# GpSimd for the low halves of the merged branches, and other places for ten weight panels, in a two-block transformer kernel

## The reference: two transformer blocks

```python
proj = h @ w_in[layer]                       # low-rank inputs, q, k, v of three attentions, gate logits
q = _rmsnorm(q, mla_q_norm_g[layer])         # per head, then rotary turning; k, and the differential
k = _rmsnorm(k, mla_k_norm_g[layer])         # attention's q1, q2, k1, k2 likewise
...
gates = jax.nn.sigmoid(gate_logits + gate_b[layer]).reshape(b, p_len, N_BRANCHES, d)
merged = (gates[:, :, 0] * (out_a @ wb_a.T)
          + gates[:, :, 1] * (out_b @ wb_b.T)
          + gates[:, :, 2] * (out_c @ wb_c.T))
h_res = h_res + merged @ w_out[layer]
```

## Time and profile before

| | |
|---|---|
| median of 3 runs | 3101.68 us (3100.57 to 3109.37) |
| the profiled execution's own time | 3117.64 us |
| its span | 3115.8 us |
| PE busy | 3059.5 us (98%) |
| DVE, ACT, POOL busy | 1938.5 us (62%), 1277.4 us (41%), 204.3 us (7%) |
| mean granted PE clock | 0.985 of full speed |

### The profile page before, as it was taken

The page is one execution under the profiler, slowest core; times in us unless marked ns, Lnnn a source line. Parts: engine busy times, 40 slices in busy tenths (PEclk is TensorE's granted clock), DMA queues, the critical chain, the costliest instruction groups (busy, mean ns, idle before and its releaser), DMA issues.

```text
span 3115.8 us, 46880 instructions
## 1 busy us (share of the span) xinstructions
PE 3059.5 (98%) x16677; PEld 2556.8 (82%) x16677; DVE 1938.5 (62%) x3719; ACT 1277.4 (41%) x2142; POOL 204.3 (7%) x350
## 2 busy tenths in 40 slices
PE   9999999999999999999999999999999999999999
PEld 7667899976779888888888888788888888877888
DVE  5555656654567787555576557755556555645775
ACT  4436565343565744222232443322223222345443
POOL 0000000000000010101010001111110111112000
PEclk9999999999999999999999999999999999999999
DMA  4222345622224564444453114455554445532454
GB/s 181 82 75 82 116 176 198 216 90 77 82 90 159 189 233 136 144 148 143 146 177 120 55 56 162 137 159 159 155 158 136 156 155 155 154 106 89 142 188 156
DMA packets 122707, 431.12 MB, mean 138 GB/s; under 512 B 16176, under 2 KB 19504, under 8 KB 122048
## 3 DMA queue, kind: packets, MB, share of 16 engines
q1 hardware_dynamic: 93776, 336.28, 31.3%
q0 software_dynamic: 26880, 86.47, 9.4%
q10 hardware_dynamic: 1904, 6.36, 0.6%
HBM read 427.99 MB, written 8.85 MB: 140 GB/s over the span
## 4 chain that ended last, share of the span: by engine, by line
PE 64%; DMA 3%; DVE 2%; ACT 1%; issue 1%; DVEq 0%; SPq 0%; ACTq 0%
PE ps L446 14%; PE ps L447 14%; PE ps L448 14%; PE ps L458 7%; PE ps L460 3%; DMA modraw<-in_mod 2%; PE ps L563 1%; PE ps L564 1%; PE ps L565 1%; PE ps L981 1%; PE ps L494 1%; PE ps L492 1%; PE ps L578 1%; PE ps L503 1%; DMA raw<-in_panels 1%; PE ps L957 1%
## 5 line engine op out<-in xcount | busy, mean ns | idle before, releaser
L1081 ACT ACTIVATE whi<-raw 128x1024 fp32r<-128x1024 f32 x632 | 668.8, 1058 | 1305.3 <-PE ps L448 808.4
L1679 DVE TENSOR_TENSOR wlo<-raw,whi 128x1024 fp32r<-128x1024 f32 x632 | 776.0, 1228 | 607.7 <-ACT whi L1081 578.5
L446 PE MATMUL ps<-xs,whi 128*128 128x512 f32 (+2 forms) x2248 | 794.5, 353 | 4.5 <-DVE wlo L1679 4.1
L448 PE MATMUL ps<-xs,wlo 128*128 128x512 f32 (+2 forms) x2248 | 780.5, 347 | 0.0
L447 PE MATMUL ps<-xs,whi 128*128 128x512 f32 (+2 forms) x2248 | 779.7, 347 | 0.0
L446 PEld LDWEIGHTS ps<-xs,whi 128*128 128x128 f32 x2248 | 427.3, 190 | 82.1 <-issue 26.4
L447 PEld LDWEIGHTS ps<-xs,whi 128*128 128x128 f32 x2248 | 427.8, 190 | 51.1 <-issue 1.0
L448 PEld LDWEIGHTS ps<-xs,wlo 128*128 128x128 f32 x2248 | 427.2, 190 | 49.8
L404 POOL DMA_DIRECT2D modraw<-in_mod x288 | 155.1, 538 | 2525.6 <-DVE modsum L1786 2359.7
L446 PE MATMUL ps<-hidden,whi 128*128 128x512 f32 (+2 forms) x838 | 294.9, 352 | 0.0
L448 PE MATMUL ps<-hidden,wlo 128*128 128x512 f32 (+2 forms) x838 | 294.8, 352 | 0.0
(11 more groups left out here) (392 smaller groups left out, 4552.1 us busy)
## 6 DMA issues: line engine op xcount, KB each, us to landing
raw<-in_panels SPq DMA_DIRECT2D x632, 512.0 KB, 3.3
modraw<-in_mod POOLq DMA_DIRECT2D x288, 256.0 KB, 3.0
bias_by_column<-in_rpb POOLq DMA_DIRECT2D x16, 476.2 KB, 8.0
bia<-bias_by_column POOLq DMA_DIRECT2D x32, 96.0 KB, 2.6
rtab<-in_rtab ACTq DMA_DIRECT2D x2, 1312.0 KB, 7.6
wuq<-in_wuq ACTq DMA_DIRECT2D x2, 768.0 KB, 6.3
con<-in_con SPq DMA_DIRECT2D x1, 1345.5 KB, 12.0
h<-in_x SPq DMA_DIRECT2D x1, 1088.0 KB, 6.5
```

What stands on the lines that cost most here:

```text
L446: pe.matmul(out, w_hi, x_hi, start=start, stop=False)
L448: return pe.matmul(out, w_lo, x_hi, start=False, stop=stop)
L1081: act.activation(whi[:, s * PW:(s + 1) * PW], raw[:, s * PW:(s + 1) * PW], ACT.Copy).then_inc(hi_split, 1)
L1679: dve.tensor_tensor(wlo[:, s * PW:(s + 1) * PW], raw[:, s * PW:(s + 1) * PW], whi[:, s * PW:(s + 1) * PW].bitcast(F32), ALU.subtract).then ...
```

## The change

It has four parts.

1. The 16 subtractions that make `mlo` (8 for each layer) go from DVE to GpSimd. Those of layer 0 stand ahead of all modulation loads in GpSimd's queue, those of layer 1 ahead of load 18. DVE now waits, ahead of the first branch of pairs 2 and 3, until GpSimd has finished with the half of `mrg` that it will write.
2. `SPREAD_FILL` goes from (4, 9, 14, 19) to (4, 9, 14, 23): filler 15 runs behind all spreads.
3. `UNIT_FILL` goes from (1, 3, 5, 7, 11, 15, 18, 20, 22) to (-1, 2, 4, 6, 9, 12, 15, 18, 21): filler 0 runs ahead of unit 0, and the other eight lie two or three units apart.
4. As a consequence of 1, the first two modulation loads are issued when layer 0's merged chunks are done, not at the start.

```diff
-UNIT_FILL = (1, 3, 5, 7, 11, 15, 18, 20, 22)
-UNIT_FILLS, SPREAD_FILL = len(UNIT_FILL) + 3, (4, 9, 14, 19)
+UNIT_FILL = (-1, 2, 4, 6, 9, 12, 15, 18, 21)
+UNIT_FILLS, SPREAD_FILL = len(UNIT_FILL) + 3, (4, 9, 14, 23)
...
+            def merged_lo(layer, m):
+
+                T, at = width1(layer), (m % 4) * T1
+                pool.wait_ge(part_hi, layer * (NC + FF1) + m + 1)
+                pool.tensor_tensor(mlo[:, m * T1:m * T1 + T], mrg[:, at:at + T], mhi[:, m * T1:m * T1 + T].bitcast(F32), ALU.subtract).then_inc(part_lo, 1)
+            for m in range(NC):
+                merged_lo(0, m)
+            first_layer_halves = 16
 
 
             n_halves = 2 * DEPTH * MODT
             for k in range(n_halves):
+                if k == first_layer_halves + 2:
+                    for m in range(NC):
+                        merged_lo(1, m)
                 s = k % 2
...
+                filler(0)
                 for u, (tens, i, p0, p1, z) in enumerate(us):
...
-                    if u in UNIT_FILL:
+                    if u in UNIT_FILL[1:]:
                         filler(UNIT_FILL.index(u))
...
-                def merged_lo(mp):
-                    for j in range(2):
-                        m, at = 2 * mp + j, (mp % 2 * 2 + j) * T1
-                        lane.take(part_hi)
-                        dve.tensor_tensor(mlo[:, m * T1:m * T1 + T], mrg[:, at:at + T], mhi[:, m * T1:m * T1 + T].bitcast(F32), ALU.subtract).then_inc(part_lo, 1)
-                    lane.count(part_lo).add(2)
+                lane.count(part_hi).add(NC)
...
                     if br == 0:
                         lane.take(gate_ready)
-                        lane.settle(part_lo)
+                        if mp > 1:
+                            lane.count(part_lo).add(2)
+                            lane.settle(part_lo)
...
-                    if br == 1 and mp:
-                        merged_lo(mp - 1)
-
...
-                merged_lo(NC // 2 - 1)
+                lane.count(part_lo).add(4)
```

## The result

| | kernel before | changed kernel |
|---|---|---|
| median of 5 runs each | 3102.71 us | 3086.68 us (3083.91 to 3090.82) |
| ratio | | 0.9944, 95% interval 0.9932 to 0.9957 |
| timed again, with the last experiments | 3107.40 us (17 runs) | 3090.14 us (6 runs), 0.9941 (0.9929 to 0.9953) |
| profiled execution: own time, span | 3117.64, 3115.8 us | 3090.82, 3089.0 us |

The change gains 16 us by the medians, 17 and 18 by the two ratios (0.0056 and 0.0059 of 3105 us). Forecast were 3082 and a gain of 20. The profiled executions differ by 26.8 us, more than the timed ones: the one of before was 15 us slower than its kernel's median. So I don't read gains from this pair alone but place by place, over the traces of all the kernels that share a place.

A forecast was written before the change was run, and what follows sets the result against it. PE bounds the kernel, its waits costing idle time and then a low clock. Terms of 22.0 us less 2.0 gave 20.0; 3101.7 less that is 3081.7, forecast 3082, range 3074 to 3096.

The forecast's parts named there:

- The start: ACT's first square: x lands earlier without two modulation loads in GpSimd's queue; 0.9 us gained, at most 1.2.
- Units: Key and first units: first-square waits and three low clock stretches go; 2.6 us in layer 0, 4.1 in layer 1.
- The term of layer 1, 4.1: Layer 1's units: 1.1 us for the first-square wait plus 3.0 for low clock stretches.
- Filler 15: Behind the spreads: no probabilities wait, next head cycle 5.12 us instead of 8.09; 3.7 us in layer 0, 3.5 in layer 1.
- The output projection: Subtractions on GpSimd remove the low-half wait and its low stretch; 3.3 us in layer 0, 3.9 in layer 1 including bank waits.
- the waits for chunks 6 and 7 that I allowed (1.2): Layer 1's output projection: 1.2 us of new PE waits for late low halves, deducted from the gain.
- the bank waits: Layer 1's branches: three quarters of PE's 1.7 us waiting for banks, 1.3, goes as DVE's queue gets shorter.
- the rival in which the clock is not regained: Half of about 13.5 us of clock gain fails to come; time 3089, chance 0.18.
- The 2.0 that the forecast took off: Whole kernel: deductions of 0.5 us for meetings and 1.5 for one low stretch, from 22.0 to 20.0.
- The 0.5 for meetings: Both layers: 0.5 us charged for GpSimd subtractions that meet DVE's splits and delay them.
- The 1.5: Whole kernel: 1.5 us deducted for one low clock stretch that new idle places may open.

The follow-up runs named there:

- after_again: The changed kernel, unaltered, timed once more against the kernel before: 3090.14 us, ratio 0.9941.
- dve_late: Changed kernel with DVE's second-head masks and a split moved behind the first head's probabilities; ratio 0.9943 against the kernel before.
- best_again: Second timing of the changed kernel with DVE's masks and split later and two modulation loads at about 80 us: 3084.63 us, 0.9929 against before.

## Why the prediction was right

**The start.** 0.9 forecast, 0.82 in the pair of traces at ACT's first square. The sum counted it as if it reached the end whole. In the same pair PE's first panel begins only 0.35 us earlier (19.20 and 18.85) and the up-projection's last matmul 0.17 earlier; in the means of all traces 0.4 is left there. So about half of the term was missing.

**Units.** The waits went as counted: the one for the first square gone, the four of 0.67 us left. The clock stayed up in all of them. The term of layer 1, 4.1, was over-sized: it took two low stretches (at 672.50 and 703 us) of one execution for lasting, and two of three traces of the same code don't have them. Layer 0 had one less than usual. In sum 5.9 against 6.7.

**Filler 15.** Shifted by the 3.1 us that layer 0 was ahead (DVE's masks end at 175.56 instead of 178.69), PE began it at 181.7 on the old axis (181.6 forecast), ended it at 187.8 (187.2), and the next two head cycles took 5.31 and 5.15 us (5.12). The start of filler 15 was right for another reason than the one given. The idle time ahead was two waits of 0.31 us, not 2 us; the rest was spreads that come no faster than one in 0.91 us at the low clock. The prediction had read 0.84 from four spreads, the first of which ran before the clock fell at 174.2 us. The second head's probabilities did not keep PE waiting. 6.2 us against 7.2: layer 0 gave 3.6 of its 3.7, layer 1 gave 2.6 of its 3.5, because in two of the five traces of the old order the heads of layer 1 had fewer low stretches and took 48.9 and 50.4 us, not 53.5 as in the one that the forecast read.

**The output projection.** In layer 0 the wait and its stretch gave 3.1 us by the time that chunks 0 to 7 of the first two panels were done (2.06 and 7.62 before, 6.62 now), where 3.3 were forecast. Then came what the sum lacked: I wrote that the two moved loads "now run at about 385, 100 us ahead of their use" and gave them no price. They took 24% of the engines' time while a ring of four waited for its panels, 1.5 us. In layer 1 the waits for chunks 6 and 7 that I allowed (1.2) did not come, another of 0.89 for `wlo` did, and the bank waits shrank by 1.3 as said. The low stretch behind the wait for `mlo` in layer 1 was no fixed cost either: with that wait at 2.3 us, the first two panels took 7.3 us in three of the five traces of the old order and 5.8 in the other two.

**The size of the whole.** The forecast's 20.0 was 12.0 of clock and 8.0 of idle time. Idle time can be read from the traces: span less busy PE was 56.3 us before, 48.0 and 46.5 in the two traces of the changed kernel, so 8.3 and 9.8 less. For the clock the timed runs are better. In the timing of after_again their mean granted clock rose from 0.9894 (17 runs) to 0.9923 (6 runs). As lost time, 0.0106 and 0.0077 of the mean spans 3105.6 and 3087.7, that is 33 and 24 us, 9 us of the 17.9 between the spans, give or take 3 by the scatter of the single clocks. So idle time came out at its terms or a little above, and the clock about 3 us short, which is no more than the error of the estimate. The two places where the forecast took the low stretches of one execution for lasting, the units and heads of layer 1, are short by 1.9 and 0.9 us, and that is the rival in which the clock is not regained, to a small degree.

Place by place the terms came to 18.7 us, not 22.0. The 2.0 that the forecast took off made up for most of that. The 0.5 for meetings was earned. The 1.5 was set aside for a low stretch at a new idle place, which the units, the heads and the projection of the changed kernel's trace don't show; that it stood in for terms which were too large was luck.

## What to carry to other kernels

Wherever a queue is rearranged, price each transfer that changes its place, at the new place: two loads of 256 KB far ahead of their use cost about 1.5 us because they landed beside panel loads that ACT already waited for. And follow a gain at the start of the program to the engine that bounds it before it is counted whole. A low stretch of the clock behind a light stretch is an event with a chance, not a fixed cost: take it from several executions, or several kernels that share the code, before it goes into a sum at its full price. And where an engine waits for a helper's queue, look at the distance at which the helper takes its turn: one number, `UNIT_LAG`, took out the 1.3 us of idle time that each layer's units had left.

## What the runs showed of the hardware

- GpSimd and DVE locked each other out in both directions. A GpSimd subtraction of 0.76 us lasted 1.76 when DVE's split was running, and DVE's two adds lasted 1.94 us instead of 0.9; DVE's instructions with one operand in PSUM were not touched (0.78 for two, beside GpSimd or not).
- The same code, with the same idle time to 0.01 us, ran its units at a clock of 1.00, 0.98 or 0.95 (69.5, 71.1 and 72.6 us, six stretches of three traces with the old table, all with 2.54 us of idle time). Executions of the kernel before spread over 16 us (3099.9 to 3116.0 in 29 runs), and the longer ones have the lower granted clock (correlation -0.86).
- The clock fell to 0.50 within the eight last spreads whether PE waited between them (two waits of 0.31 us) or not at all: small matmuls without idle time did not keep it. When it fell was not fixed: 1.2 us behind the first of them in dve_late, 4.5 us behind it in best_again, with the same order.
